# First chunk of sorted expert rows by one-hot products, and the last experts' order, in a two-layer decoder trunk

## The reference

```
g_prob = softmax(x2 @ w_group + b_group); grp = argmax(g_prob)        # 8 groups
e_logits = (x2 @ w_expert + b_expert)[group grp]                     # 8 experts in it
top_p, top_i = top_k(softmax(e_logits), 2)
weights = g_prob[grp] * top_p / sum(top_p)
order = argsort(expert_id)            # 1024 (token, expert) pairs sorted by expert
for each block of sorted rows of expert e:
    y = (silu(xb @ w_gate[e]) * (xb @ w_up[e])) @ w_down[e]
out[token] += weight * y
```

## Time and profile before

| | us |
|---|---|
| median of the runs | 1704.66 |
| profiled execution | 1703.69 |
| its span, first to last instruction | 1700.7 |
| TensorE matmuls busy | 1462.1 (86%) |
| VectorE busy | 612.1 (36%) |
| first up product of layer 0, of layer 1 | 455.85, 1209.36 |
| 128 loads of expert weights, 3072 KB each, median issue to landing | 31.6 |

### The profile page before, as it was taken

How to read it: one execution, slowest core, us unless ns; L and a number is a source line. 1 busy time by engine, 2 the same in 40 slices (tenths; PEclk the granted TensorE clock), 3 DMA queues, 4 the chain that set the end, 5 groups by cost and what they waited for, 6 DMA issues and landing times.

```text
span 1700.7 us, 24539 instructions
## 1 busy us (share of the span) xinstructions
PE 1462.1 (86%) x9187; PEld 926.3 (54%) x9187; DVE 612.1 (36%) x1520; ACT 332.4 (20%) x966; POOL 252.1 (15%) x296
## 2 busy tenths in 40 slices
PE   7999999999899777777777799999998777777776
PEld 3655466555666555545454455655865545455553
DVE  3145677743522221222214537523522222212125
ACT  2122377741210000000000235512100000000000
POOL 1121100000211111111113224000211111111112
PEclk9999999999999999999999899999999999999998
DMA  5214110042699999999998200451999999999996
GB/s 231 69 50 173 75 76 1 2 176 109 254 427 427 428 429 428 429 429 428 427 428 337 112 1 1 174 235 62 351 425 428 428 429 429 428 428 429 428 426 228
DMA packets 41280, 479.28 MB, mean 282 GB/s; under 512 B 11798, under 2 KB 12326, under 8 KB 23360
## 3 DMA queue, kind: packets, MB, share of 16 engines
q1 hardware_dynamic: 24688, 447.34, 62.4%
q0 software_dynamic: 15232, 26.35, 4.5%
q10 hardware_dynamic: 1296, 4.72, 0.8%
HBM read 460.01 MB, written 47.19 MB: 298 GB/s over the span
## 4 chain that ended last, share of the span: by engine, by line
PE 51%; DMA 39%; DVE 5%; issue 1%; ACT 1%; POOL 0%; DVEq 0%; SPq 0%; POOLq 0%; ACTq 0%
DMA sb_ring<-moe_w 26%; DMA sb_rows_space<-moe_w 10%; PE ps L1104 9%; PE ps L1292 7%; PE ps L1501 6%; PE ps L1113 5%; PE ps L1607 2%; PE ps L1637 2%; PE ps L1622 2%; PE ps L1334 2%; PE ps L1472 2%; PE ps L1365 2%; PE ps L1361 1%; PE ps L1445 1%; PE ps L1535 1%
## 5 line engine op out<-in xcount | busy, mean ns | idle before, releaser
L1104 PE MATMUL ps<-sb_ring,sb_x_block 128*64 128x256 f32 x2816 | 327.8, 386 | 83.1 <-DMA sb_ring<-moe_w 80.4
L1104 PEld LDWEIGHTS ps<-sb_ring,sb_x_block 128*64 128x64 f32 x2816 | 287.3, 198 | 160.4 <-issue 87.1
L714 POOL DMA_INDIRECT expert_rows<-sb_y_sb,sb_row_now x124 | 134.2, 1083 | 777.3 <-DVE sb_y_sb L1896 748.6
L1895 DVE COPY sb_row_now<-sb_row_of 128x1 uint32 (+1 forms) x124 | 19.0, 154 | 637.1 <-PE ps L1113 614.5
L1113 PE MATMUL ps<-sb_ring,sb_hidT 128*64 128x512 f32 x704 | 173.1, 613 | 29.8 <-ACT sb_hidT L817 29.8
L817 ACT COPY sb_hidT<-ps 128x128 f32<-128x128 f32 x128 | 33.9, 265 | 815.2 <-PE ps L1179 815.2
L1104 PE MATMUL ps<-sb_rows_space,sb_x_block 128*64 128x256 f32 x1280 | 148.5, 384 | 44.4 <-DMA sb_rows_space<-moe_w 44.4
L1104 PEld LDWEIGHTS ps<-sb_rows_space,sb_x_block 128*64 128x64 f32 x1280 | 132.3, 198 | 78.8 <-issue 60.3
L1292 PE MATMUL ps<-sb_xsT,sb_rows_space 128*128 128x512 f32 x256 | 114.7, 594 | 2.1 <-DVE sb_rows_space L2122 1.3
L1900 DVE TENSOR_TENSOR sb_x_block<-sb_xsT,sb_moe_gain 128x512 f32<-128x512 f32 x128 | 88.6, 692 | 25.2 <-issue 20.9
L1113 PEld LDWEIGHTS ps<-sb_ring,sb_hidT 128*64 128x64 f32 x704 | 43.0, 137 | 97.2 <-issue 50.9
(11 more groups left out here) (306 smaller groups left out, 1677.5 us busy)
## 6 DMA issues: line engine op xcount, KB each, us to landing
sb_ring<-moe_w SPq DMA_DIRECT2D x88, 3072.0 KB, 31.6
sb_rows_space<-moe_w SPq DMA_DIRECT2D x40, 3072.0 KB, 31.6
sb_xsT<-nsa_w_group SPq DMA_DIRECT2D x2, 2048.0 KB, 14.0
sb_ring<-nsa_w_group SPq DMA_DIRECT2D x2, 2048.0 KB, 8.0
sb_xsT<-nsa_w_out SPq DMA_DIRECT2D x1, 4096.0 KB, 12.5
kept_rows<-sb_rows_space SPq DMA_DIRECT2D x8, 512.0 KB, 2.6
token_rows<-sb_rows_space ACTq DMA_DIRECT2D x8, 512.0 KB, 2.6
sb_rows_space<-kept_rows SPq DMA_DIRECT2D x8, 512.0 KB, 26.9
```

The costliest lines, as they stand in the source:

```text
L714: pool.indirect_dma_start(out=ys_dram.rearrange("r (j n) -> (r j) n", j=2), out_offset=bass.IndirectOffsetOnAxis(ap=row_now[:, u:u + 1], a ...
L1104: last = nc.tensor.matmul(ps[j * BLOCK:(j + 1) * BLOCK, bank, 0:2 * P].rearrange("p (g n) -> p g n", g=2), x_rows[:, :, k], weights[:, 0:2 ...
```

## The change

It has four parts. The order in `rows_space` becomes x, hT, h. The first chunk of sorted rows is no longer gathered: VectorE makes one-hot columns `first_hot` from `pos`, and TensorE multiplies h in SBUF by them, 32 products, straight into the turned form. SyncE's waits ahead of experts 4 and 5 change. At the end of a stage down of expert 60 goes ahead of up of 61, and VectorE's order changes.

```diff
-        h = rows_space[:, TILES * D:2 * TILES * D]...
-        hT = rows_space[:, 2 * TILES * D:3 * TILES * D]...
+        hT = rows_space[:, TILES * D:2 * TILES * D]...
+        h = rows_space[:, 2 * TILES * D:3 * TILES * D]...
+        first_hot = sorted_space[:, 4 * P:8 * P].rearrange("p (t n) -> p t n", t=TILES)
@@ SyncE
-                sp.wait_ge(first_rows_sent, 32 * (l + 1))
                 sp.wait_ge(h_ready, TILES * (FFN_ROWS[l] + 1))
-                sp.wait_ge(h_turned, 2 * TILES * (FFN_ROWS[l] + 1))
+                sp.wait_ge(logits_done, TILES * (l + 1))
                 expert_weights(sp, l, RING, RING)...
-                for c in range(CHUNKS):
+                sp.wait_ge(rows_sent, 16 * TILES * (l + 1))
+                sp.wait_ge(chunk_turned, l * CHUNKS + 1)
+                for c in range(1, 4):
                     sp.wait_ge(rows_landed[c], 32 * l + 16)
                 expert_weights(sp, l, RING + 1, RING + 1)...
@@ GpSimd
-                for c in range(CHUNKS):
+                for c in range(1, CHUNKS):
                     pool.indirect_dma_start(out=xs_in(c), ... in_=h_dram, ...)
@@ ScalarE (VectorE likewise, with 4:8 and bank CHUNK_BANK + 1)
+                    if c == 0:
+                        nc.scalar.copy(xsT[:, 0:P, 0:4], ps[:, CHUNK_BANK, :].rearrange("p (n k) -> p n k", k=4)
+                                       ).then_inc(xsT_act, 1)
+                        return
@@ TensorE
-                keep_busy(30)
+                keep_busy(12)
...
-                turn_chunk(0)
+                pe.wait_ge(first_hot_ready, l + 1)
+                pe.wait_ge(h_ready, TILES * (FFN_ROWS[l] + 1))
+                for k in range(KD):
+                    for t in range(TILES):
+                        last = nc.tensor.matmul(
+                            ps[:, CHUNK_BANK + k // 4, :].rearrange("p (n k) -> p k n", k=4)[:, k % 4, :],
+                            h[:, t, :].rearrange("p (m k) -> p k m", k=KD)[:, k, :], first_hot[:, t, :],
+                            start=(t == 0), stop=(t == TILES - 1))
+                last.then_inc(chunk_turned, 1)
...
-                for n in range(SENT - SLOTS, SENT):
-                    if n + 1 < SENT:
-                        up(n + 1, (n + 1) % SLOTS, (n + 1) // SLOTS)
+                for n in range(SENT - SLOTS, SENT - 2):
+                    up(n + 1, (n + 1) % SLOTS, (n + 1) // SLOTS)
                     down(n, n % SLOTS, n // SLOTS)
+                n = SENT - 2
+                down(n, n % SLOTS, n // SLOTS)
+                up(n + 1, (n + 1) % SLOTS, (n + 1) // SLOTS)
+                down(n + 1, (n + 1) % SLOTS, (n + 1) // SLOTS)
@@ VectorE, in route, behind token_of
+                for t in range(TILES):
+                    step.mark(v.tensor_scalar(first_hot[:, t, :], col_no[:, :], pos[:, 0, t:t + 1], None, ALU.is_equal))
+                step.join()
+                for t in range(TILES):
+                    step.mark(v.scalar_tensor_tensor(out=first_hot[:, t, :], in0=col_no[:, :], scalar=pos[:, 1, t:t + 1],
+                                                in1=first_hot[:, t, :], op0=ALU.is_equal, op1=ALU.add))
+                step.join()
+                v.engine_nop().then_inc(first_hot_ready, 1)
@@ VectorE, end of the stage
-                add_rows(0, 0)
                 dve.wait_ge(silu_done, base + SENT + 2)
                 join_hidden(1)
-                add_rows(1, 0)
+                add_rows(0, 0)
                 keep_here(1)
                 add_rows(0, 1)
                 add_kept(0)
+                add_rows(1, 0)
                 add_rows(1, 1)
                 add_kept(1)
```

More of the change, by code:

```diff
@@ L129, in build @@
         x = rows_space[:, 0:TILES * D].rearrange("p (t n) -> p t n", t=TILES)
-        h = rows_space[:, TILES * D:2 * TILES * D].rearrange("p (t n) -> p t n", t=TILES)
-        hT = rows_space[:, 2 * TILES * D:3 * TILES * D].rearrange("p (k n) -> p k n", k=KD)
+        hT = rows_space[:, TILES * D:2 * TILES * D].rearrange("p (k n) -> p k n", k=KD)
+        h = rows_space[:, 2 * TILES * D:3 * TILES * D].rearrange("p (t n) -> p t n", t=TILES)
         gain = sb("gain", [P, D])
@@ L220, in build @@
         scratch = xsT[:, :, :].rearrange("p n k -> p (n k)")
-        h_space = rows_space[:, TILES * D:2 * TILES * D]
-        hT_space = rows_space[:, 2 * TILES * D:3 * TILES * D]
+        hT_space = rows_space[:, TILES * D:2 * TILES * D]
+        h_space = rows_space[:, 2 * TILES * D:3 * TILES * D]
         tri = sb("tri", [P, P])
@@ L421, in build @@
         inverted = sem("inverted")
-        first_rows_sent = sem("first_rows_sent")
-        last_rows_sent = sem("last_rows_sent")
         x_kept = sem("x_kept")
+        first_hot_ready = sem("first_hot_ready")
+        rows_sent = sem("rows_sent")
         moe_gain_loaded = sem("moe_gain_loaded")
@@ L563, in mla_loads @@
                 for c in range(CHUNKS):
-                    sp.wait_ge(rows_landed[c], 32)
+                    sp.wait_ge(rows_landed[c], 32 if c else 16)
                 sp.wait_ge(down_done, EXPERTS - 2)
@@ L693, in moe_moves @@
                 pool.wait_ge(token_ready, l + 1)
-                pool.wait_ge(first_rows_sent, 32 * (l + 1))
-                pool.wait_ge(last_rows_sent, 32 * (l + 1))
-                for c in range(CHUNKS):
+                pool.wait_ge(rows_sent, 16 * TILES * (l + 1))
+                for c in range(1, CHUNKS):
                     pool.indirect_dma_start(
@@ L787, in send @@
                         act.wait_ge(h_ready, TILES * FFN_ROWS[layer] + t + 1)
-                        act.dma_start(h_dram[t * P:(t + 1) * P, :], h[:, t, :]).then_inc(
-                            first_rows_sent if t < 2 else last_rows_sent, 16)
+                        act.dma_start(h_dram[t * P:(t + 1) * P, :], h[:, t, :]).then_inc(rows_sent, 16)
                     for t in range(TILES):
@@ L1906, in chunk_half @@
                     dve.wait_ge(chunk_turned, l * CHUNKS + c + 1)
+                    if c == 0:
+                        nc.vector.tensor_copy(xsT[:, 0:P, 4:8], ps[:, CHUNK_BANK + 1, :].rearrange("p (n k) -> p n k", k=4)
+                                              ).then_inc(xsT_dve, 1)
+                        return
                     nc.vector.tensor_copy(xsT[:, c * P + BLOCK:(c + 1) * P, :].rearrange("p n k -> p (n k)"),
@@ L1983, in add_rows @@
                     c = k * TILES + t
-                    dve.wait_ge(rows_landed[c], 32 * l + 32)
+                    dve.wait_ge(rows_landed[c], 32 * l + 32 if c else 16 * l + 16)
                     if k == 0:
```

## The result

The changed kernel took 1713.36 us, the median of five runs (1711.96 to 1713.89), against 1703.08 us for the kernel before in the same comparison (five runs, 1700.25 to 1704.96). The ratio is 1.0054, 95% interval 1.0041 to 1.0067: slower by some 9 us, where 9 us faster was forecast. The profiled execution's span is 1712.0 us against 1700.7.

What follows compares the result with a forecast made beforehand. The prediction took the weight stream, DMA at 428 GB/s, to bound each MoE stage. Gains of 3.4 - 0.3 + 0 + 3.4 + 2.4 = 8.9 us from 1703.69 gave 1694.8, median 1695.8, stated as 1695.5; range 1690 to 1701.5.

Steps and rivals of the forecast that it cites:

- Part 1: MoE start, first chunk by products: 7.4 us product; TensorE's chain 3.2 us earlier in layer 0, 2.4 later in layer 1.
- The bound on top, 14.8: Upper bound in us on the first chunk's product in the MoE start, for TensorE at the lower clock.
- rival C: MoE start: chunk product runs at the lower clock, 14.8 us, 7.4 more, so 1710 us in all; chance 0.05.
- e: Microseconds the chunk product takes beyond forecast; each costs e in layer 1 and e - 0.8 in layer 0.
- Two of the signs: Forecast wrong if the chunk product takes over 9 us, or layer 1's stream starts over 1.5 us later.
- The 3.1 us that the forecast gave to the two starts: MoE starts of both layers: 3.4 us gained in layer 0, 0.3 us lost in layer 1.
- Part 2: Slot 5's weight load at the MoE start goes out 7.6 us earlier in layer 0, 6.3 in layer 1.
- the forecast loss of 0.3: Layer 1's weight stream: TensorE frees slots late, so expert 8 lands at 1250.6 against 1250.3, 0.3 us lost.
- Part 3: Last sent experts, down of 60 before up of 61: taken as 0 (0.5 lost to 1.5 gained, both layers).
- Part 4: VectorE's order at each MoE stage's end: 3.4 us gained in layer 0, 2.4 in layer 1.
- Rival B: Stage ends: VectorE and GpSimd hinder each other; layer 0 gains 1.0, layer 1 1.5; 1699 us; chance 0.14.
- Rival A: MoE start: slot 5's load holds up gathers of chunks 4 to 7, each 7 us more; 1699 us; chance 0.13.

Runs made afterwards that it cites:

- e5_host_order: Changed kernel with gate and up weights and gain laid out in the input so that reads of h take neighbouring columns: 1696.77 us, ratio 0.9965.
- e8b_host_end_late: e7_all_gathered without the early load (slot 5's load stays behind all gathers): 1697.34 us, ratio 0.9971 to the kernel before.
- e1_end_only: Kernel before with only the new order of the last experts and VectorE's new order at the end: 1700.67 us, ratio 0.9977.
- e7_all_gathered: Kernel before with the outside weight order, slot 5's load behind four gathers and the changed end; all eight chunks gathered, no product: 1694.70 us, ratio 0.9943.
- e6: Kernel before with one edit, slot 5's load waiting for four gathers instead of eight: 1701.53 us, ratio 0.9992.
- e9: e7_all_gathered with slot 5's load waiting for one gather instead of four: 1705.51 us, ratio 1.0014 to the kernel before.

## Why the prediction was wrong
**Part 1 failed, in one term: "The chunk is 64 instructions, 7.4 us", at the 0.116 us of a filler each.** It measured 15.48 us, 0.242 each. The price was taken from the fillers, which have the same shape but another operand layout. The up products of the same kernel had the product's layout, and the group of their weight loads would have pointed at it: 64 spread columns in 198 ns against 137 for neighbours. (The pace of the up products would not: 32 of their instructions take 3.74 us, as 32 fillers would.) The bound on top, 14.8, was there for another reason (the lower clock) and so got 0.05. The Trainium skill has the rule in SBUF — State Buffer, "Specifications (TRN2)": lines of 16 bytes, of which each wants at least two accesses for full bandwidth. By it the product's columns, at most one to a line, are read slowly; it gives no size. The runs agree on where the cost begins (7.63 us at 16 bytes apart, 3.93 at 8), and they alone show the factor of two. The prediction did not weigh it: it read the change as instructions of a shape, not as access patterns.

**From there everything follows by the prediction's own sum.** It said of rival C that e more costs e in layer 1 and e - 0.8 in layer 0. With e = 15.48 - 7.4 = 8.1 the streams are worth +7.3 - 3.4 = 3.9 and 8.1 + 0.3 = 8.4; measured +4.4 and +9.5. TensorE's first up product was forecast at 454.4 and came at 464.41, 10.0 later: 8.1, the 1.7 that arose before, and 0.25 of handing over. So rival C had the place, the size and nearly the result (1710 against 1713.4), with a wrong cause: the clock granted over both products was 1.00. That a halved clock and spread columns both cost a factor of two is luck. Two of the signs that the prediction gave for being wrong showed: a product over 9 us, and a stream of layer 1 that starts late.

**Part 1's other steps were right.** VectorE's eight operations took 2.0 us (1.9 forecast). With the columns as neighbours the product took 7.41. In that kernel (`e5_host_order`) the first up product came, counted from the keeping of x, 1.2 us earlier in layer 0 and 2.6 later in layer 1, where 1.45 and 2.4 were forecast. Its streams changed by -3.8 and +0.2 us where -3.4 and +0.3 were forecast, but that agreement proves nothing: in `e8b_host_end_late`, with no product and no early load, they changed by -4.2 and +0.1. There the gathers of layer 0 began 14.3 us after the keeping of x and in `before` 17.6, with no edit ahead of them, so layer 0's stream in a single profile carries some 3 us of chance. The 3.1 us that the forecast gave to the two starts are not shown by any run.

**Part 2.** The load went out when the product was done, at 462.81 and 1222.33, as that was the later of the two waits. Counted from the keeping of x that is 3.0 us earlier than before in layer 0 and 1.9 later in layer 1, where 7.6 and 6.3 earlier were forecast. It gave nothing, as expert 8's load then waited for its slot. In `e5_host_order` it went out at 457.05, near the forecast (456.4, with the product starting 2.2 later than forecast). An early load alone is worth little (0.9992); that it is so because in layer 1 the slots are freed late is argued, as for the forecast loss of 0.3, not shown.

**Part 3** was put at nothing and cannot be told apart from part 4; it was not run alone.

**Part 4 was right in mechanism and near in size.** Forecast: 3.4 and 2.4 gained. After: 3.1 and 2.1; alone (`e1_end_only`): 3.2 and 3.3, with 3.9 us (1.7 to 6.0) in the ratio. These rows of the kernel after answer to the earlier trace rows:

```profile
937.10 1.28 DVE L2015 SCALAR_TENSOR_TENSOR sb_rows_space<-sb_rows_space,sb_sent_wt 128x1024 f32<-128x1024 f32 x1 [6.63 <-DMA sb_rows_space<-expert_rows,sb_pos_u]
...
939.16 6.56 PE L1269 MATMUL ps<-sb_y_sb,sb_xsT 64*128 64x512 f32 x16 [4.87 <-DVE sb_y_sb L2002]
939.55 1.61 POOL L729 DMA_INDIRECT sb_rows_space<-expert_rows,sb_pos_u  x1 [0.30 <-issue]
941.36 1.22 DVE L2020 TENSOR_TENSOR sb_rows_space<-sb_rows_space,ps 128x1024 f32<-128x1024 f32 x1 [1.06 <-PE ps L1269]
...
946.28 1.28 DVE L1708 SCALAR_TENSOR_TENSOR sb_rows_space<-sb_rows_space,sb_rstd,sb_gain 128x1024 f32<-128x1024 f32 x1
...
1690.75 1.94 PE L1117 MATMUL ps<-sb_ring,sb_hidT 128*64 128x512 f32 x8 [0.36 <-ACT sb_hidT L817]
```

From the landed rows to the sums are 2.06 us (937.10 to 939.16), where it was 7.02 (930.36 to 937.38), and to the first addition of kept rows another 2.2, as said. In layer 1 the down product is back at 1.94 us. Rival B is there but small: a gather instruction took 1.61 us and the second norm operation of tile 0 1.38 instead of 0.58, yet its result was ready at 945.55, and the scaling of tile 0 follows VectorE's additions at 946.28 without a wait for GpSimd.

**Rival A** could not show in the kernel after, whose load came 5 us or more behind the last gather. It is real, and its "7 us more" for a gather is what was measured (6.7 to 14.0); the 4 us that the prediction worked out beside it are too few. Sent 6 us earlier, the load costs 12 us in both layers. The prediction's reason against it, that all gathers have been issued before the load goes out, does not hold as it stands: in `e5_host_order` the last gather, issued 0.8 us ahead of the load, took 14.5 us. It did little harm in layer 0, as TensorE came to that chunk late enough to wait only 0.19 us for it.

## What to carry to other kernels
- Price a product by its access patterns, not its shape: fp32 products of 128x128 by 128 ran at half rate with the stationary columns 16 or 32 bytes apart, or with the moving operand 32 bytes apart. So look for a row of the same layout before taking one of the same size. Where a price is to be trusted, open the weight-load groups of every line that shares the layout.
- A load brought forward holds up the gathers behind it and those issued up to 1.5 us ahead of it. Count which chunks those are and when they are wanted: with one late gather the kernel gained 9.7 us, with five it lost 2.
- A change of several parts is worth splitting: here the part that looked like tidying (the order at the end) gave 3.9 us by itself, and the clever part (the product) lost more than that through its layout and gave nothing that can be told with the layout repaired.

## What of the hardware was not expected
- The cost of distance is a step, not a slope: 3.74, 3.93, 7.63, 7.81 us for columns 4, 8, 16 and 32 bytes apart. The PSUM output 16 bytes apart cost 3.84, close to nothing. The transposes of each chunk, whose stationary operand (64x128) had its columns 32 bytes apart, took 1.14 us for 16, and 0.71 with neighbours (`before` and `e7_all_gathered`).
- ScalarE slowed down as well with a spread output: 2.04 to 2.10 us instead of 1.13 to 1.15 for 128x1024, with its elements written 512 bytes apart.
- One 3 MB load doubled the time to landing of the gathers around it at the same total rate. In the four kernels with an early load and a trace read for it (`e5`, `e6`, `e7`, `e9`), gathers issued 1.75 us or more ahead of the load landed in 4.4 to 8.3 us, those issued 1.5 us ahead or less, or behind it, in 12.7 to 15.6.
